# Two modulation blocks weighted on ScalarE and added on GpSimd, and expert weights loaded in pairs of chunks

## The reference, cut to what matters

```python
# first block; c and c_ctx are vectors of 1024, w_mod is 1024 x 6144
mod_x = (silu(c) @ w_mod + b_mod).reshape(-1, 6, d)
mod_c = (silu(c_ctx) @ w_mod[:, :2 * d] + b_mod[:2 * d]).reshape(1, 2, d)
hx = rms_norm(x, g_mix) * (1 + mod_x[:, 1]) + mod_x[:, 0]
hc = rms_norm(ctx, g_mix) * (1 + mod_c[:, 1]) + mod_c[:, 0]
x = x + mod_x[:, 2] * hybrid_mixer(hx, hc, w_in, ...)   # retention, window and neighbourhood attention
hx = rms_norm(x, g_ffn) * (1 + mod_x[:, 4]) + mod_x[:, 3]
x = x + mod_x[:, 5] * expert_choice_ffn(hx, ...)        # 16 experts, each takes its 32 best tokens
# one expert: hid = silu(xe @ w_gate) * (xe @ w_up); ye = hid @ w_down, each matrix 1024 x 1024
# second block: a sparse attention layer and a recurrent layer, each with a gated FFN,
# and 12288 columns of modulation (ada_w) of their own
```

## Time and profile before

| | |
|---|---|
| median of 3 runs | 1810.52 us (1806.41 to 1811.04) |
| profiled execution, its own time | 1809.85 us |
| profiled execution, its span | 1807.8 us |
| granted TensorE clock, mean | 0.887 |
| busy: TensorE, VectorE, ScalarE, GpSimd | 84%, 44%, 32%, 2% of the span |
| DMA | 437.95 MB, 242 GB/s mean |

### The profile page before, as it was taken

How to read it: one execution, slowest core, us unless ns; L and a number is a source line. 1 busy time by engine, 2 the same in 40 slices (tenths; PEclk the granted TensorE clock), 3 DMA queues, 4 the chain that set the end, 5 groups by cost and what they waited for, 6 DMA issues and landing times.

```text
span 1807.8 us, 27194 instructions
## 1 busy us (share of the span) xinstructions
PE 1523.9 (84%) x11250; PEld 1156.5 (64%) x11250; DVE 787.8 (44%) x1166; ACT 579.6 (32%) x834; POOL 33.8 (2%) x39
## 2 busy tenths in 40 slices
PE   6999997799976676666666799888999989889999
PEld 3788874568842111121211688447999989779999
DVE  4352345466641101010101755545555475865653
ACT  4332034475321000000001531544333354743332
POOL 2000020000000000000000000000000000100000
PEclk8999998899967776676767897989999999889999
DMA  9655455543729999999999452952455534335540
GB/s 393 247 220 193 155 214 215 201 164 112 304 93 422 422 421 421 421 422 421 422 420 422 187 188 91 359 200 94 170 182 185 187 140 167 136 117 187 187 164 24
DMA packets 60573, 437.95 MB, mean 242 GB/s; under 512 B 6736, under 2 KB 6992, under 8 KB 7600
## 3 DMA queue, kind: packets, MB, share of 16 engines
q1 hardware_dynamic: 59616, 430.99, 61.3%
q0 software_dynamic: 560, 5.01, 0.7%
q10 hardware_dynamic: 288, 0.32, 0.1%
HBM read 435.25 MB, written 1.05 MB: 241 GB/s over the span
## 4 chain that ended last, share of the span: by engine, by line
PE 44%; DMA 21%; DVE 8%; ACT 3%; issue 2%; SPq 1%; PEld 0%; PEldq 0%; DVEq 0%; ACTq 0%
PE bank L653 41%; DMA ring<-in_w 21%; PE bank L989 2%; DVE ring_r L1609 1%; PE bank L657 1%; SPq L559 1%; DVE arena L1912 1%; ACT ring_r L1299 1%; DVE norm_t L1562 1%; PE bank L1015 0%; DVE arena L2034 0%; ACT arena L1453 0%; DVE arena L1870 0%; DVE H L1599 0%; DVE arena L2035 0%
## 5 line engine op out<-in xcount | busy, mean ns | idle before, releaser
L653 PE MATMUL bank<-H_r,ring_r 128*128 128x256 f32 x3488 | 510.6, 288 | 18.5 <-DVE H_r L1586 18.5
L653 PEld LDWEIGHTS bank<-H_r,ring_r 128*128 128x128 f32 x3488 | 465.4, 196 | 24.0 <-issue 22.6
L653 PE MATMUL bank<-arena_r,ring_r 128*128 128x256 f32 x2776 | 400.9, 288 | 30.4 <-DVE ring_r L1609 24.5
L1609 DVE TENSOR_TENSOR ring_r<-ring,ring_r 128x2048 fp32r<-128x2048 f32 x136 | 319.3, 2350 | 235.5 <-ACT ring_r L1299 235.2
L653 PEld LDWEIGHTS bank<-arena_r,ring_r 128*128 128x128 f32 x2776 | 371.9, 195 | 47.6 <-issue 23.2
L1299 ACT ACTIVATE ring_r<-ring 128x2048 fp32r<-128x2048 f32 x136 | 259.5, 1909 | 218.8 <-PE bank L653 174.9
L989 PE MATMUL bank<-ring,arena 128*32 128x512 f32 x1024 | 197.7, 866 | 108.4 <-DMA ring<-in_w 106.4
L989 PEld LDWEIGHTS bank<-ring,arena 128*32 128x32 f32 x1024 | 25.8, 126 | 265.2 <-DMA ring<-in_w 227.2
L1870 DVE TENSOR_TENSOR arena<-arena,bank 64x512 f32<-64x512 f32 x16 | 11.1, 692 | 289.0 <-ACT arena L1401 289.0
L1401 ACT ACTIVATE arena<-bank 64x512 f32<-64x512 f32 x16 | 9.4, 588 | 372.3 <-PE bank L989 372.3
L1015 PE MATMUL bank<-ring,arena 128*32 128x256 f32 x1024 | 85.7, 487 | 21.4 <-DMA ring<-in_w 13.6
(11 more groups left out here) (245 smaller groups left out, 1267.6 us busy)
## 6 DMA issues: line engine op xcount, KB each, us to landing
ring<-in_w SPq DMA_DIRECT2D x408, 1024.0 KB, 10.5
ring<-in_bias POOLq DMA_DIRECT2D x1, 2048.0 KB, 10.8
consts<-in_consts POOLq DMA_DIRECT2D x1, 1439.0 KB, 9.9
X<-in_x SPq DMA_DIRECT2D x1, 1024.0 KB, 5.3
arena<-in_ctx SPq DMA_DIRECT2D x1, 1024.0 KB, 7.8
arena<-in_decay POOLq DMA_DIRECT2D x1, 1024.0 KB, 11.7
out_t<-X SPq DMA_DIRECT2D x4, 256.0 KB, 2.0
wide<-in_wide POOLq DMA_DIRECT2D x1, 256.0 KB, 11.8
```

Of the source, the lines that this page charges most:

```text
L653: i = nc.tensor.matmul(o, lhsT, rhs, start=start, stop=stop, skip_group_check=grouped)
L1609: v.tensor_tensor(r(lo), lo, r(hi), ALU.subtract).then_inc(lo_ready, 1)
```

## The change

1. Blocks 1 and 2 are no longer multiplied chunk by chunk. ScalarE scales each chunk in place by silu of its row of c (the first of a block straight into a new tile `mod_acc`, 128 x 2048, in arena room that the values `v_n` use later); GpSimd adds the other seven into `mod_acc`; and at the eighth step TensorE multiplies `mod_acc` with a matrix of ones, four matmuls for the block. A weighing stands in the list of steps two chunks ahead of its own.
2. TensorE's `mod` step of these blocks now waits for the weighing or the addition, and counts the chunk as used.
3. The expert chunks are loaded two at a time, into two neighbouring slots, 16 KB a partition, from a stream laid out for it. A pair is issued when the earlier contents of both slots have been used, and both halves wait for one landing.

```diff
+WEIGH_AHEAD = 2
...
-            fills[s] = fills.get(s, 0) + 1
-            places.append((s, fills[s], last.get(s)))
+            sem_slot = s
+            if FIRST_EXPERT <= c < FIRST_SECOND:
+                sem_slot = s - s % 2
+            if sem_slot == s:
+                fills[s] = fills.get(s, 0) + 1
+            places.append((s, fills[sem_slot], last.get(s), sem_slot))
...
+    for c, x in enumerate(CHUNKS):
+        if x[0] == "mod" and 0 < x[1] < ADD_BLOCKS:
+            before.setdefault(CHUNKS[c - WEIGH_AHEAD], []).append(("mod_weigh",) + x[1:])
...
+        mod_acc = room(11264, CHUNK)
...
+            def load_pair(s, source):
+                sp_eng.dma_start(ring[:, s:s + 2, :].rearrange("p a b -> p (a b)"), source).then_inc(landed[s], 16)
...
+                with sp_eng.Fori(1, full) as r:
+                    for i in range(SLOTS // 2):
+
+                        sp_eng.wait_ge(chunk_used, r * SLOTS + (FIRST_EXPERT + 2 * i + 2 - SLOTS))
+                        load_pair(2 * i, source[r, i])
...
+            for blk in range(1, ADD_BLOCKS):
+                for k in range(1, KT):
+                    c = CHUNK_NO[("mod", blk, k)]
+                    eng.wait_ge(mod_weighed, (blk - 1) * KT + k + 1)
+                    if k > 1:
+                        eng.wait_ge(mod_added, (blk - 1) * (KT - 1) + k - 1)
+                    nc.gpsimd.tensor_tensor(mod_acc, mod_acc, ring[:, slot_of(c), :], ALU.add).then_inc(mod_added, 1)
...
             def step_mod(blk, k):
 
+                if 0 < blk < ADD_BLOCKS:
+
+                    pe.wait_ge(mod_weighed if k == 0 else mod_added, (blk - 1) * (KT if k == 0 else KT - 1) + max(k, 1))
+                    if k == KT - 1:
+                        begin(("mod_row", blk))
+                        for j in range(4):
+                            mm(mods[32 * j:32 * j + 32, :], ones[:, 0:32], mod_acc[:, 512 * j:512 * j + 512], True, True,
+                               mod_done if j == 3 else None)
+                    owed[0] += 1
+                    return
...
+            def step_mod_weigh(blk, k):
+                c = CHUNK_NO[("mod", blk, k)]
+                ck = ring[:, slot_of(c), :]
+                act.wait_ge(landed[slot_of(c)], 16 * landed_count(c))
+                if k == 0 and blk > 1:
+
+                    act.wait_ge(mod_done, blk)
+                f(mod_acc if k == 0 else ck, ck, ACT.Copy, scale=silu_c[:, 2 * k:2 * k + 1]).then_inc(mod_weighed, 1)
```

More of the change, by code:

```diff
@@ L41 @@
 SLOTS = 12
-MOD_BLOCKS, LAST_BLOCKS = 9, 6
+MOD_BLOCKS, LAST_BLOCKS, ADD_BLOCKS = 9, 6, 3
 PAIRS, LAG = 16, 2
@@ L228, in landed_count, with landed_slot @@
     return RING[c][1]
+def landed_slot(c):
+    return RING[c][3]
 def with_splits(steps):
@@ L491, in build @@
         x_final = sem("x_final")
+        mod_weighed, mod_added = sem("mod_weighed"), sem("mod_added")
         sp_arg, sp_exp, sp_ready = sem("sp_arg"), sem("sp_exp"), sem("sp_ready")
@@ L559, in load, with pair_of, pair_rounds @@
                 sp_eng.dma_start(ring[:, s, :], source).then_inc(landed[s], 16)
+            def load_pair(s, source):
+                sp_eng.dma_start(ring[:, s:s + 2, :].rearrange("p a b -> p (a b)"), source).then_inc(landed[s], 16)
+            def pair_of(c):
+                return w[c:c + 2].rearrange("t p f -> (t p f)").rearrange("(q x) -> q x", q=P)
+            def pair_rounds():
+                full = EXPERTS * 12 // SLOTS
+                source = w[FIRST_EXPERT:FIRST_SECOND].rearrange("(r s t) p f -> r s (t p f)", s=SLOTS // 2, t=2)
+                source = source.rearrange("r s (q x) -> r s q x", q=P)
+                with sp_eng.Fori(1, full) as r:
+                    for i in range(SLOTS // 2):
+                        sp_eng.wait_ge(chunk_used, r * SLOTS + (FIRST_EXPERT + 2 * i + 2 - SLOTS))
+                        load_pair(2 * i, source[r, i])
             def rounds(stage):
@@ L588, in _ @@
             sp_eng.wait_ge(merged_ready, 4)
[L589 to L594, removed]
+            for s in range(6, SLOTS, 2):
+                load_pair(s, pair_of(FIRST_EXPERT + s))
+            for s in RING_USE[1][1][::2]:
+                for half in range(2):
+                    sp_eng.wait_ge(chunk_used, RING[FIRST_EXPERT + s + half][2] + 1)
+                load_pair(s, pair_of(FIRST_EXPERT + s))
             sp_eng.wait_ge(chunk_used, FIRST_EXPERT)
-            for s in RING_USE[1][2]:
-                load(s, w[FIRST_EXPERT + s])
-            rounds(2)
+            load_pair(RING_USE[1][2][0], pair_of(FIRST_EXPERT + RING_USE[1][2][0]))
+            pair_rounds()
             for i, s in enumerate(RING_USE[3][1]):
@@ L986, in step_experts @@
                         c = FIRST_EXPERT + 12 * e + k
-                        pe.wait_ge(landed[slot_of(c)], 16 * landed_count(c))
+                        pe.wait_ge(landed[landed_slot(c)], 16 * landed_count(c))
                         for j in range(4):
@@ L1009, in step_experts @@
                         s = KT + c
-                        pe.wait_ge(landed[s], 16 * landed_count(FIRST_EXPERT + 12 * e + s))
+                        at = FIRST_EXPERT + 12 * e + s
+                        pe.wait_ge(landed[landed_slot(at)], 16 * landed_count(at))
                         ck = ring[:, s, :].rearrange("p (k n) -> p k n", k=2)
@@ L1515, in _ @@
                      "router": step_router, "pick": step_pick, "gather": step_gather,
-                     "experts": step_experts, "mod_row": step_mod_row, "nkv": step_nkv, "nqk": step_nqk,
+                     "experts": step_experts, "mod_row": step_mod_row, "mod_weigh": step_mod_weigh, "nkv": step_nkv, "nqk": step_nqk,
                      "nnorm": step_nnorm, "ngate": step_ngate, "cmp": step_cmp, "cmp_s": step_cmp_s,
@@ L2129, in weight_stream @@
                 w[c, :, j * P:(j + 1) * P] = rg[g, k * P:(k + 1) * P, n * P:(n + 1) * P]
+    for c in range(FIRST_EXPERT, FIRST_SECOND, 2):
+        w[c:c + 2] = w[c:c + 2].transpose(1, 0, 2).reshape(2, P, CHUNK).copy()
     return w
```

## The result

The changed kernel took 1831.93 us (median of 4 runs, 1829.97 to 1834.18) and the kernel before 1808.47; the ratio on record is 1.0122 [1.0103, 1.0141] (95% interval; the two medians alone give 1.0130), slower by 23 us. The profiled execution took 1833.31 us with a span of 1831.5, against 1809.85 and 1807.8 before.

A forecast was written before the change was run, and what follows sets the result against it. It took TensorE to bound the first mixer and DMA loads the expert part, with a tight six-slot ring between. Mixer 25, block 2 -3.5 and experts -3.8 made +17.7 on 1809.85: 1827.5 us, range 1807 to 1842.

The forecast's parts named there:

- The start: Before `kr` 0: ScalarE's two weighings delay `mod_out` 0's bias to 43.1, +7.9 us; GpSimd's addition holds VectorE's 16th subtraction, +4.5.
- The first ring cycle: Behind `kr` 0: TensorE waits 9 us for weighings and additions; `qr` 0 starts at 88.5, ends +18.4 late; clock loses 1.5.
- `decay_m` and `vr` 0: Next two ring cycles: additions hold VectorE, splits end at 101.7 and 113.4, +21.5 and +25.9 late; `mod_row` 1 +29.5.
- I count each of the two second additions by half, 2 x 2.2: +25: Block 1's cycles: unknown whether GpSimd's second addition goes first, so the mixer's lateness is taken as +25, not +29.5.
- The sum below would be the same: `decay_m` step: if its first operation (L1640) also waits, nothing changes, as the two-input one behind waits anyway.
- Block 2: Modulation from 114 to 162 us: seven steps saved give -6.5, held VectorE operations cost some 3; -3.5 in all.
- four such places give some 3 us: Block 2: additions in the way of split chains cost 2.2 each on average, 1.2 spare; some 3 us, bounds 0 and 8.
- Behind it every stage hangs on the one before: After the first mixer: nothing absorbs its lateness of +21.5 us.
- The experts: Expert loads: larger packets give -6, half of -12; later release 0.9 and end 1.3 against it: -3.8, bounds -10 and +2.5.
- The exclusion costs little: Rival, mixer: GpSimd's additions fall into VectorE's gaps or VectorE gets in first; +0.3, 1810 us, no change; chance 0.14.
- Faster, by the larger packets: Rival, expert part: 16 KB packets give 9.8 us and the mixer loses less than 5; 1804 us; chance 0.11.
- Still slower: Rival: each addition holds a VectorE operation, block 2 stalls by 8, pairs bring nothing; +33.5, 1843 us; chance 0.10.

The follow-up runs named there:

- Experiment 3: Changed kernel with single expert loads, its first two weighings moved behind the first `apply`, ahead of `kr` 0: 1824.55 us against 1837.25 without the move.
- adds_beside: Kernel before plus 14 GpSimd additions of `mod_acc` to itself, each started by a landed modulation chunk, no step waiting until `vn`: 1820.76 us, ratio 1.0061.
- pairs_only: Changed kernel without weighed blocks, so the kernel before with expert loads in pairs of 16 KB packets: 1805.66 us, ratio 0.9982 to the kernel before.
- experiment 4: Changed kernel with single expert loads (1837.25 us): fills replacing GpSimd's additions, 1817.39; additions on VectorE, 1820.86. Kernel before with unneeded GpSimd additions: 1820.76.
- mod_only_late_start: Changed kernel with single expert loads and the first two weighings behind the first `apply`, ahead of `kr` 0: 1824.55 us, ratio 1.0083 to the kernel before.

## Why the prediction was right, and what it mis-sized

It said 1827.5 us, slower by a start, held VectorE operations and a slow first ring cycle; 1831.93 came out, inside its range, by that mechanism. That the forecast is no further off is in part luck: errors of both signs stand in it.

- **The start, +7.9 and +4.5.** Measured 43.72 for 43.1, and a subtraction held until GpSimd's 4.49 us addition was over. Experiment 3 gives 12.7 for the 12.4. Right.
- **The first ring cycle, `qr` 0 at 88.5.** It came at 89.5, with TensorE still for 8.5 us. Right in place and size. "1.5 us of work lost" to the clock was 2.9 there. The prediction has the clock in this one place only; over the mixer the work lost to it grew by 8.8 us, from 5.1 to 13.9. How much of that lay on the path is not shown.
- **`decay_m` and `vr` 0.** `qr` 1's subtraction started at 99.60 and `vr` 0's ended at 113.33; the walk had 99.4 and 113.4, with the operations held by (1, 4) and (1, 5). `mod_row` 1 was 29.7 late by the rotation behind it (132.00 against 102.31), and the walk had 29.5.
- **The term that was mis-sized: "I count each of the two second additions by half, 2 x 2.2: +25".** GpSimd was first both times, so the whole walk of +29.5 came true and the halving took 4.5 us off for nothing. On the spans, 23.7 came for 17.7: 4.5 of the 6.0 are this term, and the others (block 2, the stretch behind the mixer, the experts) leave 1.5.
- **"The sum below would be the same" if L1640 waits too.** It did wait (L1698, 4.74 us), and that was not without effect on the sum: it bears on whether a second addition comes in. A VectorE operation that already waits goes ahead of GpSimd's next addition, in `adds_beside` at 69.51 and in the changed kernel between (2, 6) and (2, 7): L1748 ended at 194.28, 0.28 us behind the first of them, and only then came the second, which held L1750 until 199.04. In `decay_m` 0 the operation that waited was the short first one; (1, 4) went behind it, ahead of the second. Had the first not been held, the second would have been the one in waiting and ahead of (1, 4), so this hold is what let the second addition in. That last step is argued from these rows; no run frees L1698 alone.
- **Block 2, -3.5.** It gave 4.4: 7.4 less busy, 3.0 more idle; the prediction had 6.5 and 3. Right. Its "four such places give some 3 us" is 4 by its own figures of 2.2 less 1.2, and VectorE was held for 17.0 us there.
- **"Behind it every stage hangs on the one before."** The lateness went from 25.6 at 248 us to 28.4 at the experts. The other kernels, which all do the same work there, moved by -5.7 to +3.8 over that stretch, so this 2.8 is given no cause.
- **The experts, -3.8.** The lateness fell from 28.4 at the first hidden row to 22.3 at VectorE's first L1870 behind them (994.45 and 1016.74). It was 23.4 at the norm that follows, as TensorE's clock was 0.50 from 1018 to 1020 and 1.00 in the kernel before: -5.0 in all. Of 12 us that a 16 KB packet promised at face value the prediction took half; the rate of 428 for 421 makes 1.6% of 437, 7 us. `pairs_only` as a whole gained 3.3.
- **The rivals.** "The exclusion costs little" fell with experiment 4, at 19.9 us. "Faster, by the larger packets": the packets do it, by the mechanism named, but at a fifth of what the mixer lost. "Still slower" had each addition hold a VectorE operation and block 2 stall by 8. Holds there were in both blocks (20.4 and 17.0 us), but in block 2 TensorE stood still for 3.0 us only, and pairs did bring something. That the start or the exclusion alone could be the cause fell as well: each correction leaves a kernel that is slower than before.

The terms as measured are 25.6 for the mixer, 2.8 up to the experts, -5.0 there and +0.3 behind: 23.7, the growth of the span.

## What to carry to other kernels

Before moving an addition to GpSimd, look which two-input or fast one-input VectorE operations stand on a chain beside it: here a 0.75 us operation on the path cost 4.9. The one that already waits goes first, so of two VectorE operations that depend on each other each can pay one of two GpSimd additions in a row. Count that in full, not by half. Work put into an engine's list in fixed order must stand behind the first result that others wait for. A saving on the busiest engine counts only in the stretch in which that engine is the bound: the same edit lost 30 us where the ring was tight and gained 4 to 6 where TensorE was full, and the better version weighs block 2 alone, with its additions on VectorE.

## What the runs showed of the hardware that was not expected

- The rate of a load stream follows the packet even above 8 KB: 421, 428 and 431 GB/s for 8, 16 and 32 KB, with 1, 2 and 4 MB transfers; 2 MB transfers in 8 KB packets stayed at 421. The Trainium skill (DMA: Bandwidth & Descriptors, "Measured") gives rates by the size of the transfer, 341 GB/s for 1 MB and 425 for 16 MB, issued from GpSimd. In this stream from SyncE's queue 1 and 2 MB in packets of 8 KB both ran at 421, so no effect of the size shows between these two.
- Turns alternate. Of two dependent VectorE operations (L1698, L1699), both were held, 4.74 and 4.92 us, by two GpSimd additions in a row: the first ran between them, and the second found GpSimd at work again. L1748 and L1750 in block 2 did the same (4.52 and 4.72 us, where each takes 0.42 when nothing holds it).
- The hold goes both ways. GpSimd's addition took 4.49 us with nothing in its way, but 5.91 at 166.28, where VectorE's subtraction of 161.19 was still running until 167.78, 1.50 us into it; and 6.04 in `mod_only_late_start` at 49.56, 1.58 us ahead of the end of a subtraction. The mean of the 14 was 4.80 us. GpSimd's fills of 128 x 2048 took 1.82 us.
